# Dropping the 32 spare columns from the routed rows that TensorE holds in the expert stage

## The reference, cut to what matters

```python
def expert_choice_ffn(h, w_router, w_gate, w_up, w_down):
    B, T, D = h.shape
    n = B * T
    cap = max(1, EC_FACTOR * n // N_EXPERTS)      # 32 for the prompt, 64 for the sample
    xt = h.reshape(n, D)
    aff = jax.nn.softmax((xt @ w_router).astype(jnp.float32), axis=-1)
    gates, idx = lax.top_k(aff.T, cap)
    xe = xt[idx]
    a = jnp.einsum('ecd,edf->ecf', xe, w_gate)    # D = 1024, f = 2048
    u = jnp.einsum('ecd,edf->ecf', xe, w_up)
    ye = jnp.einsum('ecf,efd->ecd', jax.nn.silu(a) * u, w_down).astype(jnp.float32)
    ye = ye * gates[..., None]
    out = jnp.zeros((n, D), jnp.float32).at[idx.reshape(-1)].add(ye.reshape(-1, D))
    return out.reshape(B, T, D)
```

## Time and profile before

| what | value |
|---|---|
| median of 3 runs | 1552.45 us (1550.77 to 1552.91) |
| the profiled execution's own time | 1552.91 us |
| span from its first to its last instruction | 1551.1 us |
| mean granted TensorE clock, as a share of full speed | 0.985 |
| TensorE busy | 1492.5 us (96%) |
| VectorE busy | 1252.7 us (81%) |
| ScalarE busy | 1065.4 us (69%) |
| expert stage | from 455.9 us to the end |

### The profile page before, as it was taken

How to read it: one execution, slowest core, us unless ns; L and a number is a source line. 1 busy time by engine, 2 the same in 40 slices (tenths; PEclk the granted TensorE clock), 3 DMA queues, 4 the chain that set the end, 5 groups by cost and what they waited for, 6 DMA issues and landing times.

```text
span 1551.1 us, 18383 instructions
## 1 busy us (share of the span) xinstructions
PE 1492.5 (96%) x7228; PEld 1221.5 (79%) x7228; DVE 1252.7 (81%) x1144; ACT 1065.4 (69%) x1133; POOL 127.7 (8%) x103
## 2 busy tenths in 40 slices
PE   6998998999949999999999999999999999999997
PEld 5786777667838888888888888888888888888885
DVE  5359588786478898988889898888989888898985
ACT  7434335676347778787877877787787877778784
POOL 1023122000000001000000000000000101000000
PEclk9999999999969999999999999999999999999999
DMA  7111011401749999999999999999999999999992
GB/s 244 55 55 55 1 55 55 151 28 55 258 138 373 390 356 387 386 378 395 378 394 378 384 386 376 395 375 394 380 384 388 375 394 379 391 383 381 393 375 65
DMA packets 192069, 448.49 MB, mean 289 GB/s; under 512 B 12976, under 2 KB 13296, under 8 KB 191984
## 3 DMA queue, kind: packets, MB, share of 16 engines
q1 hardware_dynamic: 187440, 433.03, 74.9%
q0 software_dynamic: 3968, 12.65, 3.6%
q10 hardware_dynamic: 576, 1.64, 0.3%
HBM read 434.71 MB, written 12.58 MB: 288 GB/s over the span
## 4 chain that ended last, share of the span: by engine, by line
PE 90%; DVE 5%; issue 2%; ACT 1%; DMA 1%; POOL 0%; POOLq 0%; DVEq 0%; ACTq 0%
PE ps L910 23%; PE ps L912 23%; PE ps L911 23%; PE ps L591 5%; PE ps L593 5%; PE ps L592 5%; PE ps L945 1%; PE ps L806 1%; PE ps L840 1%; DVE t L1445 1%; DVE states L1430 1%; PE ps L903 1%; PE ps L826 1%; PE ps L862 1%; DMA ident<-in_ident 0%
## 5 line engine op out<-in xcount | busy, mean ns | idle before, releaser
L1752 DVE TENSOR_TENSOR wl<-raw,wh 128x2048 fp32r<-128x2048 f32 x384 | 873.5, 2290 | 127.6 <-ACT wh L1279 126.2
L1279 ACT CAST wh<-raw 128x2048 fp32r<-128x2048 f32 x384 | 731.2, 1913 | 127.6 <-PE ps L912 125.4
L910 PE MATMUL ps<-wh,XTh 128*128 128x512 f32 x1024 | 405.9, 396 | 0.6 <-issue 0.6
L912 PE MATMUL ps<-wl,XTh 128*128 128x512 f32 x1024 | 400.3, 391 | 0.0
L911 PE MATMUL ps<-wh,XTl 128*128 128x512 f32 x1024 | 399.5, 390 | 0.0
L912 PEld LDWEIGHTS ps<-wl,XTh 128*128 128x128 f32 x1024 | 192.8, 188 | 41.3
L910 PEld LDWEIGHTS ps<-wh,XTh 128*128 128x128 f32 x1024 | 192.9, 188 | 38.9 <-issue 0.9
L911 PEld LDWEIGHTS ps<-wh,XTl 128*128 128x128 f32 x1024 | 193.1, 189 | 38.3
L910 PE MATMUL ps<-wh,gTh 128*128 128x512 f32 x512 | 200.9, 392 | 1.2 <-DVE gTl L1763 1.2
L912 PE MATMUL ps<-wl,gTh 128*128 128x512 f32 x512 | 199.4, 390 | 0.0
L911 PE MATMUL ps<-wh,gTl 128*128 128x512 f32 x512 | 199.2, 389 | 0.0
(11 more groups left out here) (238 smaller groups left out, 1519.3 us busy)
## 6 DMA issues: line engine op xcount, KB each, us to landing
raw<-in_w_gate SPq DMA_DIRECT2D x128, 1024.0 KB, 11.0
raw<-in_w_up SPq DMA_DIRECT2D x128, 1024.0 KB, 11.5
raw<-in_w_down SPq DMA_DIRECT2D x128, 1024.0 KB, 11.4
slice_raw<-in_w_in SPq DMA_DIRECT2D x6, 2048.0 KB, 8.0
X<-in_x_sample SPq DMA_DIRECT2D x8, 512.0 KB, 12.6
slice_raw<-in_w_out SPq DMA_DIRECT2D x2, 2048.0 KB, 9.2
X<-in_x_prompt SPq DMA_DIRECT2D x4, 512.0 KB, 5.0
h_rows<-hn SPq DMA_DIRECT2D x4, 512.0 KB, 3.3
```

Of the source, the lines that this page charges most:

```text
L910: pe.matmul(out, hi, rhs_h, start=first, stop=False)
L912: return pe.matmul(out, hi, rhs_l, start=False, stop=last)
L1279: act.copy(wh[:, n % CONV, :], raw[:, n % RAW, :]).then_inc(s_wh, 1)
L1752: dve.tensor_tensor(wl[:, n % CONV, :], raw[:, n % RAW, :], wh[:, n % CONV, :].bitcast(F32), ALU.subtract).then_inc(s_wl, 1)
```

## The change

The held operands become exactly 96 columns wide, the matmuls write 96 rows of PSUM, and the clearing of the spare columns goes away with its semaphore. The tiles shrink from 4 KiB to 3 KiB a partition (2 KiB to 1.5 KiB for the hidden rows) and are placed anew; `XTh0` and `XTl0` leave a place far from their partners (131072 and 135168) for one beside them.

```diff
-        gTh = at("gTh", 180224, [P, FC, P], F32R)
-        gTl = at("gTl", 182272, [P, FC, P], F32R)
-        hid = at("hid", 184320, [P, FS])
-        XTh = [at("XTh0", 131072, [P, KD, P], F32R), at("XTh1", 192512, [P, KD, P], F32R)]
-        XTl = [at("XTl0", 135168, [P, KD, P], F32R), at("XTl1", 196608, [P, KD, P], F32R)]
+        gTh = at("gTh", 180224, [P, FC, CAP], F32R)
+        gTl = at("gTl", 181760, [P, FC, CAP], F32R)
+        hid = at("hid", 183296, [P, FS])
+        XTh = [at("XTh0", 185344, [P, KD, CAP], F32R), at("XTh1", 195584, [P, KD, CAP], F32R)]
+        XTl = [at("XTl0", 192512, [P, KD, CAP], F32R), at("XTl1", 198656, [P, KD, CAP], F32R)]
...
-            pool.wait_ge(s_lg, NT)
-            pool.memset(XTh[0][:, :, CAP:P].bitcast(F32), 0.0)
-            pool.memset(XTl[0][:, :, CAP:P].bitcast(F32), 0.0)
-            pool.memset(gTh[:, :, CAP:P].bitcast(F32), 0.0)
-            pool.memset(gTl[:, :, CAP:P].bitcast(F32), 0.0).then_inc(s_pad, 1)
             for b in range(2):
                 pool.wait_ge(s_h2w[b], 16 * (NT // 2))
-            pool.memset(XTh[1][:, :, CAP:P].bitcast(F32), 0.0)
-            pool.memset(XTl[1][:, :, CAP:P].bitcast(F32), 0.0).then_inc(s_pad, 1)
             pool.wait_ge(s_route, 1)
             gather(0)
...
-                        mm = products(ps[:, b, :], (XTh[j][:, kk, :], XTl[j][:, kk, :]),
+                        mm = products(ps[0:CAP, b, :], (XTh[j][:, kk, :], XTl[j][:, kk, :]),
...
-                        mm = products(ps[:, 4 + half, :], (gTh[:, ff, :], gTl[:, ff, :]),
+                        mm = products(ps[0:CAP, 4 + half, :], (gTh[:, ff, :], gTl[:, ff, :]),
...
-            pe.wait_ge(s_pad, 2)
...
-                act.copy(XTh[e % 2][:, 4 * half:4 * half + 4, 0:CAP],
+                act.copy(XTh[e % 2][:, 4 * half:4 * half + 4, :],
...
-                act.copy(gTh[:, :, 0:CAP], ps[:, 6, 0:FC * CAP].rearrange("p (f c) -> p f c", f=FC)).then_inc(s_gth, 1)
+                act.copy(gTh[:], ps[:, 6, 0:FC * CAP].rearrange("p (f c) -> p f c", f=FC)).then_inc(s_gth, 1)
```

More of the change, by code:

```diff
@@ L299, in build @@
         s_out = sem("residual_stored")
-        s_pad = sem("spare_columns_cleared")
         s_issued = sem("first_gather_issued")
@@ L1756, in xt_copy @@
                 dve.wait_ge(s_xth, 2 * e + (half + 1))
-                dve.tensor_tensor(XTl[e % 2][:, 4 * half:4 * half + 4, 0:CAP],
+                dve.tensor_tensor(XTl[e % 2][:, 4 * half:4 * half + 4, :],
                                   ps[:, rows_bank(e, half), 0:4 * CAP].rearrange("p (k c) -> p k c", k=4),
-                                  XTh[e % 2][:, 4 * half:4 * half + 4, 0:CAP].bitcast(F32), ALU.subtract).then_inc(s_xtl, 1)
+                                  XTh[e % 2][:, 4 * half:4 * half + 4, :].bitcast(F32), ALU.subtract).then_inc(s_xtl, 1)
             def turned(q):
                 dve.wait_ge(s_gth, q + 1)
-                dve.tensor_tensor(gTl[:, :, 0:CAP], ps[:, 6, 0:FC * CAP].rearrange("p (f c) -> p f c", f=FC),
-                                  gTh[:, :, 0:CAP].bitcast(F32), ALU.subtract).then_inc(s_gtl, 1)
+                dve.tensor_tensor(gTl[:], ps[:, 6, 0:FC * CAP].rearrange("p (f c) -> p f c", f=FC),
+                                  gTh[:].bitcast(F32), ALU.subtract).then_inc(s_gtl, 1)
             dve.wait_ge(s_issued, 1)
```

## The result

The changed kernel takes 1567.92 us (median of 4 runs, 1567.23 to 1568.79) against 1552.56 us: a ratio of 1.0105, interval 1.0093 to 1.0116. It is 15.4 us slower. The forecast was 1550.3 us with a range to 1559. Rival B had said 1568.7.

The account below looks back on a forecast made before the run. The prediction took TensorE's matmul spacing in the expert stage to bound the kernel. Only the shorter loads behind turnings counted, 2.2 us, all else nothing: 1552.45 - 2.2 = 1550.3 us, range 1539 to 1559.

Parts of the forecast that it names:

- Rival B: Expert stage: spacing doesn't settle with 96 columns, staying 4.0 ns longer, 18.4 us lost, 1568.7 us; chance 0.11.
- What bounds the kernel: Expert stage: TensorE sets the pace, so time is 4608 matmuls times their 226.7 ns spacing, 1044.6 us.
- I take no change of spacing: Expert-stage products: 96 held columns leave the 226.7 ns between matmul starts as it is, 0 us.
- Places: Moving `XTh0` beside the rest is worth nothing, since odd and even experts take 67.63 and 67.64 us today.
- Behind a turning: First product after rows are turned: its uncovered load gets 27 ns shorter, 80 times, 2.2 us gained.
- Memsets, copies, waits: GpSimd's six memsets, ScalarE's copy into `gTh` and TensorE's 1.2 us wait for `gTl`: nothing gained.
- two bounding rows: Low-rank projection, 64 and 32 held columns alternating: 3.3 ns saved at 256 streamed columns, 4.0 ns lost at 512.
- A: Expert stage: narrower loads shorten the spacing itself, 1534.9 us in full or 1544.2 us by columns; chance 0.20.
- C: Held-operand loads: 96 columns load slower than 128, costing 8.8 us behind the turnings, 1561.3 us; chance 0.04.
- D: Expert stage: the granted clock falls because fewer columns work, about twice the stage's time; chance 0.01.

Follow-up runs that it names:

- Experiment 1: Kernel before with matmuls holding 96 columns and writing 96 PSUM rows, tiles, places and memsets unchanged: 1562.44 us, ratio 1.0068.
- the sweep: Kernel before with another number of held columns for each expert, from 128 down to 16: 1563.4 us in one run.
- experiment 4: Kernel before with each expert's held gate and up operands placed differently, expert 6 with 128 columns and slices 384 bytes apart: 1561.56 us in one run.
- Experiment 2: Changed kernel with slices still 384 bytes apart, but matmuls holding 128 columns and tiles 128 bytes longer: 1574.65 us, ratio 1.0148.
- experiment 7: Kernel before, only uncovered loads behind turnings 96 wide, turnings moved: 1562.27 us (128 wide everywhere: 1564.99); with the second turning mended, 1548.94 us.

## Why the prediction was wrong, point by point

- **What bounds the kernel** was right. That made the spacing the one term that counts, as the prediction says at its end: 1 ns is 4.6 us.
- **The step that failed** is "I take no change of spacing". It measured 4.17 ns, 18.9 us. I had the price in the earlier trace rows, 4.0 ns and 18.4 us, from the only rows with narrow loads and 512 streamed columns, and set it aside because two widths alternate there. Experiment 1 shows that a constant 96 costs 3.3 ns as well (230.0 against 226.7), and the sweep that every narrower width tried has a longer mean (227.8 to 233.9 ns). The other reason, that equal loads following one another give 13.3 ns on top, was read from two rows that were both 128 wide and both aligned; it says nothing about other widths.
- **I saw one of two causes.** Under "Places" I took the equal pace of odd and even experts as proof that the place is worth nothing. Both buffers start on multiples of 512 bytes with slices 512 bytes apart, so the rows could not show what slices 384 bytes apart do. Expert 6 of experiment 4 does: 232.2 ns at 128 columns. Experiment 2, which also moves the starts of the low tiles, costs 23 us. In the changed kernel, where the width has already broken the rhythm, the places take the mean spacing from 230.0 to 231.4 ns: 15.4 us over the kernel before, against 10.9 in experiment 1.
- **Behind a turning**: 27 ns and 2.2 us forecast, 28.7 ns and 2.3 us measured; experiment 7 gains 2.6 to 2.7 us when nothing else is lost, of which only 24 ns a turning, 1.9 us, are the load; the quicker settling was not foreseen. Loads of 161 ns forecast, 161 to 162 measured.
- **Memsets, copies, waits** were worth nothing, as forecast: the wait for `gTl` is 1.2 us in both kernels, ScalarE's copy 480 ns against 481.
- **The rivals.** B had the place, the mechanism as far as rows could tell it, and the size (1568.7 against 1567.9). It should have had far more than 0.11: of the two bounding rows it rested on the one nearer to the case. That its size fitted so well is luck: 4.0 ns came from 64 and 32 columns in turn with all tiles aligned, while of the 4.17 ns here the width alone brings 2.7 (230.0 against 227.3) and the places the rest, which B did not have; other widths cost between 0.5 and 6.6 ns more than 128 in the sweep. A's row was true, but for 256 streamed columns. C wants a longer load; the loads from 16 to 128 columns stay on one line, 95 to 188 ns, so it didn't occur. D didn't either. The rule of the Trainium skill ("TensorE: Matmul & The Clock Gate", "Weight-path perf modes — Fast Weight Load (FWL) and DoubleRow") that the fast load wants the full 128 columns had the sign of the result, but not as its cause: at 128 no load here is fast (188 ns, against 186 at 126 columns).

What stays open: why a spacing settles at all. Shown is that it settles at 13.3 ns over the streaming time when 128 columns are held and both operands start alike within 256 bytes; that otherwise it runs through longer values, in many of the kernels in a fixed cycle (four spacings in experiment 1, seven with all held tiles moved by 128 bytes); that 124, 88 and, at one place, 96 columns hold the settled value in some stretches and not in others; and that the loads' duration is not the cause. Why it is so, and why these widths, no run here shows.

## What to carry to other kernels

Where TensorE bounds a kernel, measure the distance between starts and not durations, and ask of each change to an operand's shape, also one that removes work, whether that distance stays. Don't pack held operands tightly to save bytes: a spare quarter of the columns was free here, and leaving it out cost 1%. Let the slices of both operands start alike within 256 bytes. Narrow a load only where it isn't covered, as behind a turning.

## What the runs showed of the hardware that was not expected

- A stream of matmuls with 512 streamed columns has a settled spacing of 226.7 ns and unsettled ones, with means from about 228 to 235 ns a stretch; 126 held columns are slower (233.3) than 128 or 96 (230.0).
- Held and streamed operand 128 bytes apart in their alignment: 1575 us; both moved by 128 bytes: 1552 us; the held one moved by 256: 1552 us.
- The rhythm depends on what went before: 96 columns at one place ran at 226.7 ns behind a settled stream, and for the first 59 spacings of a kernel that was that wide throughout, but at 231.7 ns behind its turnings.
- At 88 and 124 held columns the same products ran settled in some stretches (226.7 ns) and not in others.
